# Hybrid decoder block on eight cores: one input tile held back, PSUM copies moved to VectorE, LayerNorm statistics paced at two a step

## The reference

```python
u = rms_norm(h, mix_pre_g)
proj = u @ w_in                                  # 1024 -> 5120
u_glu = proj[..., :2048]; p = proj[..., 2048:3072]
gates = sigmoid(proj[..., 3072:])                # g_conv, g_pool
y_conv = conformer_conv_branch(u_glu, ...)       # GLU, depthwise conv 31, LayerNorm, swish, @ w_conv_out
y_pool = pooling_branch(p, ...)                  # trailing means 2, 4, 8, 16 minus token, group linear, @ w_pool_out
h = h + rms_norm((g_conv * y_conv + g_pool * y_pool) @ w_o, mix_post_g)
v = rms_norm(h, mlp_pre_g)
v = square(relu(v @ w_ff1)) @ w_ff2
h = h + rms_norm(v, mlp_post_g)
```

## Time and profile before

| | us |
|---|---|
| median of the runs shown | 975.74 (975.29 to 1109.9) |
| the profiled execution | 976.0 |
| its span on the slowest core (7) | 974.4 |
| spans of the eight cores | 971.7 to 974.4 |
| TensorE busy on core 7 | 949.2 (97%) |
| VectorE busy | 451.3 (46%) |
| ScalarE busy | 277.6 (28%) |

### The profile page before, as it was taken

How to read it: one execution, slowest core, us unless ns; L and a number is a source line. 1 busy time by engine, 2 the same in 40 slices (tenths; PEclk the granted TensorE clock), 3 DMA queues, 4 the chain that set the end, 5 groups by cost and what they waited for, 6 DMA issues and landing times.

```text
span 974.4 us, 14114 instructions; the slowest of 8 cores (971.7 to 974.4 us)
## 1 busy us (share of the span) xinstructions
PE 949.2 (97%) x4971; PEld 484.2 (50%) x4971; DVE 451.3 (46%) x767; ACT 277.6 (28%) x531; POOL 62.6 (6%) x112
## 2 busy tenths in 40 slices
PE   7789999999999999999999999999999999999996
PEld 4655666665545544444444444444444444444444
DVE  4478886575482114566666630344223431244222
ACT  4553111132114431333335530233202330133211
POOL 1010001000010000121213200000000000000000
PEclk9999999999999999999999999999999999999999
DMA  9995165976780021759989995220022001210021
GB/s 183 253 146 74 17 89 105 143 109 115 118 140 1 1 87 15 143 117 191 168 190 178 196 197 90 87 87 1 1 87 87 1 1 44 87 43 1 1 86 66
DMA packets 93111, 91.21 MB, mean 94 GB/s; under 512 B 43601, under 2 KB 74577, under 8 KB 92914
## 3 DMA queue, kind: packets, MB, share of 16 engines
q0 software_dynamic: 32416, 35.13, 26.2%
q1 hardware_dynamic: 60626, 55.18, 21.1%
HBM read 98.88 MB, written 16.84 MB: 119 GB/s over the span
## 4 chain that ended last, share of the span: by engine, by line
PE 91%; DMA 3%; DVE 3%; ACT 1%; issue 1%; DVEq 0%; ACTq 0%; SPq 0%
PE ps L220 90%; DMA arena<-w_in 2%; DMA arena<-xh 1%; ACT arena L238 1%; PE ps L223 1%; DVE arena L246 1%; DVE arena L250 1%; DVE arena L477 0%; DMA arena<-arena 0%; DVE arena L241 0%; ACT sm L238 0%; DVE arena L256 0%; DVEq L159 0%; DVE sm L400 0%; ACTq L159 0%
## 5 line engine op out<-in xcount | busy, mean ns | idle before, releaser
L220 PE MATMUL ps<-arena 128*128 128x512 bf16 (+4 forms) x4731 | 937.9, 360 | 13.9 <-DVE arena L246 2.8
L220 PEld LDWEIGHTS ps<-arena 128*128 128x128 bf16 (+1 forms) x4731 | 470.1, 103 | 473.4 <-issue 25.7
L238 ACT ACTIVATE arena<-ps 128x512 bf16<-128x512 f32 (+5 forms) x346 | 203.0, 593 | 622.1 <-PE ps L220 467.0
L246 DVE TENSOR_SCALAR ps<-ps 128x512 f32<-128x512 f32 x128 | 89.1, 699 | 110.9 <-PE ps L220 110.2
L241 DVE TENSOR_TENSOR ps<-ps,arena 128x512 f32<-128x512 f32 (+1 forms) x65 | 43.6, 688 | 176.1 <-ACT arena L238 175.6
L250 DVE SCALAR_TENSOR_TENSOR arena<-arena,ps 128x512 bf16<-128x512 f32 (+1 forms) x64 | 43.9, 686 | 133.0 <-ACT arena L238 111.0
L241 DVE TENSOR_TENSOR arena<-ps,arena 128x512 bf16<-128x512 f32 (+2 forms) x52 | 42.3, 830 | 35.6 <-ACT arena L238 29.6
L238 ACT ACTIVATE arena<-arena 128x1024 bf16<-128x1024 f32 (+1 forms) x33 | 34.8, 1054 | 46.3 <-DVE arena L250 35.8
L250 DVE SCALAR_TENSOR_TENSOR arena<-ps,sm,arena 128x512 f32<-128x512 f32 (+1 forms) x65 | 45.1, 737 | 5.0 <-DVE sm L400 3.0
L250 DVE SCALAR_TENSOR_TENSOR arena<-arena,sm 128x1024 bf16<-128x1024 f32 (+1 forms) x33 | 42.3, 1282 | 4.3 <-POOL sm L396 2.4
L241 DVE TENSOR_TENSOR arena<-arena 128x512 bf16<-128x512 f32 (+2 forms) x56 | 38.4, 690 | 4.3
(11 more groups left out here) (34 smaller groups left out, 91.3 us busy)
## 6 DMA issues: line engine op xcount, KB each, us to landing
arena<-xh SPq DMA_DIRECT2D x32, 512.0 KB, 8.6
arena<-w_ff POOLq DMA_DIRECT2D x16, 1024.0 KB, 27.8
out<-arena SPq DMA_DIRECT2D x31, 512.0 KB, 3.1
arena<-out SPq DMA_DIRECT2D x16, 512.0 KB, 4.1
arena<-w_in POOLq DMA_DIRECT2D x12, 512.0 KB, 13.1
arena<-w_in POOLq DMA_DIRECT2D x2, 2048.0 KB, 17.2
arena<-gb SPq DMA_DIRECT2D x4, 512.0 KB, 6.4
arena<-w_pool_out POOLq DMA_DIRECT2D x2, 1024.0 KB, 23.1
```

Source lines behind the costliest of these rows:

```text
L220: kb.op("pe", lambda e: e.matmul(o, lhsT=l, rhs=r, start=start, stop=stop), [l, r], [o])
L238: kb.op("act", lambda e: e.activation(out=o, in_=i, func=func, **kw), rd, wr)
L246: kb.op("dve", lambda e: e.tensor_scalar(out=o, in0=a, scalar1=s1, scalar2=s2, op0=op0, **kw), rd, [o])
```

## The change

Three edits. SyncE issues x tile 0 (the third after 2 and 3) only when tile 3 has landed. All copies of the units with u = 2 and 3 go to VectorE; in the same list of calls, the 14 warm matmuls ahead of unit (0,1) become 6 ahead of it and 8 behind unit (1,1), and units (2,1) and (3,1) come before the transposes of tiles 1 and -1. The background queue gives up two items a step in place of three.

```diff
-                          after=[wev[j - 4]] if j in (4, 5, 6) else [])
+                          after=[wev[j - 4]] if j in (4, 5, 6) else [xev[3]] if j == 0 else [])
...
-                p_group(cc, 256 * u, 256, "dve" if u > 1 and cc % 2 else "act")
+                p_group(cc, 256 * u, 256, "dve" if u > 1 else "act")
...
-        do([(warm, 6), (nrm, 2), (setup,), (nrm, 3), (trn, 2), (warm, 3), (nrm, 0), (trn, 3), (nrm, 1), (nrm, -1), (warm, 14),
-            (pu, 0, 1), (pu, 1, 1), (trn, 0), (trn, 1), (trn, -1), (pads,), (pu, 2, 1), (pu, 3, 1),
+        do([(warm, 6), (nrm, 2), (setup,), (nrm, 3), (trn, 2), (warm, 3), (nrm, 0), (trn, 3), (nrm, 1), (nrm, -1), (warm, 6),
+            (pu, 0, 1), (pu, 1, 1), (warm, 8), (trn, 0), (pu, 2, 1), (pu, 3, 1), (trn, 1), (trn, -1), (pads,),
             (pu, 0, 0), (pu, 1, 0), (pu, 2, 0), (pu, 3, 0), (pu, 4, 1), (pu, 4, 0), (nrm, 4), (pu, 5, 1), (pu, 5, 0),
             (nrm, 5), (pu, 6, 1), (pu, 6, 0), (pu, 7, 1), (trn, 4), (pu, 7, 0), (trn, 5), (nrm, 6),
             (pu, 0, 2), (pu, 1, 2), (pu, 2, 2), (nrm, 7), (trn, 6), (pu, 3, 2), (pu, 4, 2), (nrm, 8), (pu, 5, 2),
...
-                pump(3)
+                pump(2)
```

## The result

The changed kernel takes 982.91 us (median of 981.4 to 983.55) where the kernel before, run beside it on the same chip, takes 975.67: a ratio of 1.0073, with a 95% interval of 1.0053 to 1.0093. By the ratio the change costs 7.1 us (0.1% is 0.98 us); the forecast was 974.4, in a range of 972.0 to 977.8. The profiled execution took 983.55 us. The changed kernel is slower, clear of noise, though by less than 2%.

A forecast was written before the change was run, and what follows sets the result against it. TensorE was taken to set the pace from 58 us, so an earlier start of the 512-token blocks moves the end. Slowest span 1.3 us shorter: 976.0 - 1.3 - 0.26, about 974.4 us; range 972.0 to 977.8.

The forecast's parts named there:

- Part 1: Holding x tile 0 until tile 3 lands: first weight piece at 15.5 to 16 us, second unchanged; no gain so far.
- queued behind it: On SyncE behind held x tile 0: tiles 1 and -1, vec, and tile 4, which waits for the first weight piece anyway.
- S: Start of the third token block, unit (0,2): 38.42 us before on core 7, forecast 37.55; core 4 forecast 37.75.
- 400 packets: Weight packets brought forward in 1.5 us of having the engines alone, worth 1.2 us at the full rate.
- Part 2: New projection order: unit (6,1) at 31.4 us on core 7, 0.6 later; earlier tile 4 still brings the third token block forward.
- half clock at (2,1): Rival, chance 0.1: 1.5 us TensorE idle after transpose 0 halves the clock at unit (2,1), costing 1.3 us; time 975.7.
- Part 3: Eight copies moved from ScalarE to VectorE: third token block to 512-token blocks 17.9 us against 19.74, 1.9 us less.
- G: Start of the 512-token projection blocks: 58.16 us before on core 7, forecast 55.45; core 4 56.67, forecast 55.65.
- Nothing: Rival, chance 0.1: transposes of tiles 8 to 11 land when they did; core 4's 512-token blocks do not move; 975.7.
- The idle at *G: Rival, chance 0.15: idle ahead of the 512-token blocks shrinks from 2.64 to 2.0 us, clock stays full; 1.3 us more, 973.1.
- Part 4: Two statistics a step, four moved into the last two steps: price 0, at most 1.4 us if VectorE's idle were gone.

The follow-up runs named there:

- the hold alone: Kernel before, with only x tile 0's issue held until x tile 3 has landed: 979.26 us, ratio 1.0031.
- order alone: Kernel before, with only the new order of warm matmuls (6 ahead of unit (0,1), 8 behind (1,1)), units and transposes: 978.16 us, ratio 1.0027.
- order with all 14: Kernel before, with units (2,1), (3,1) ahead of the transposes of tiles 1 and -1, all 14 warm matmuls still ahead of (0,1): 976.58 us, ratio 1.0008.
- the copies alone: Kernel before, with only the copies of units u = 2 and 3 all on VectorE: 977.22 us, ratio 1.0012.
- memsets: Kernel before, with sixteen small one-element memsets added on VectorE and nothing else: 978.04 us, ratio 1.0028.

## Why the prediction was wrong

- **The failed step: Part 1, "queued behind it".** The prediction listed what stands behind the held transfer on SyncE, and stopped there. The waiting goes on: behind the transfer stands ScalarE's square, behind it VectorE's reciprocal and product, and behind these, on VectorE, tile 3's copy, for which unit (0,1) waits. "Their transposes now stand behind more work" was true of tile 0's own and said nothing of tile 3's. Instead of about 16 us, (0,1) started at 21.32, and *S* came at 44.38 instead of 37.55. In the changed kernel, moving tile 3's copy ahead brought 5.0 of the 7.1 us back; with the hold alone the late tiles' transposes, ahead of (2,1), took its place.
- **Part 1, the size of the delay.** "Later by one to three us" for tile 0; it is 5.6: the chain has it from 9.40 to 17.30, 7.9 us in flight, beside 3.4 us for a tile into idle queues, and before it was in at 11.7. While it is in flight the weights move too, and they gain what the tiles lose: SyncE issues tile 4, which waits for the first piece, at 12.27 us, 5.0 earlier than before (17.27) and ahead of the bounds of 13.8 to 17.2. The "400 packets" were too few. The second piece stayed, as said (19.3 to 20.7).
- **Part 2.** From (2,1) to (6,1) it takes 10.8 us (27.53 to 38.33) and from there to *S* 6.05; the prediction had 10.85 and 6.15, and the copy wait of 0.85 us at (0,0) is there. Right in itself, on a start that was 7 us late.
- **The rival "half clock at (2,1)"** was the right kind and got 0.1. Its place was wrong (ahead of (0,1), not behind it) and so was its price: the 24 matmuls took 5.92 us where full clock makes them 3.6: 2.3 us, not 1.3. Moving eight warm matmuls behind (1,1) costs 1.9 us by itself (order alone against order with all 14). The rule of the Trainium skill that the prediction named ("TensorE: Matmul & The Clock Gate", Part 1: the throttled clock is the default, activity lifts it) agrees: 0.50 behind the idle of 3.76 us that six warm matmuls leave.
- **Part 3** came out in the changed kernel, in part by luck: *S* to *G* is 18.03 us (17.9 forecast, 19.74 before), VectorE is busy 16.52 of these 18.1 us, the wait of 2.35 us on ScalarE is gone, the idle ahead of *G* is 2.31 us. But this is at an *S* nearly 7 us late, with the DMA engines at 0.70 in that stage against 1.02 before. At about the *S* that was forecast (the copies alone, 36.5 to 38.6 us) tile 8's transpose landed 4 to 5 us later after *S*, and 17.9 held on two cores of eight. The rival "Nothing" describes core 4 there: tile 8's transpose lands at 52.81 us, before at 52.84, and *G* moves by 0.2 us. The idle at *G* did not drop enough: 2.1 to 2.5 us, with the half clock on six cores of eight behind it, as before. What failed is the claim that the stages behind *G* stay as long as before: the moved copies shift VectorE's pause into the eight scalings. No row of the prediction showed TensorE's idle there, though its 1.85 us were in the trace, right behind the last of the earlier trace rows.
- **Part 4** was right: price 0.
- **The range.** Each rival was priced alone and added to a start taken as safe. Its upper end, 977.8, holds one mishap; here the queue, the clock and the pause came together. The sum for core 7 misses by 62.41 - 55.45 = 7.0 us at *G* and by 3.3 us behind it (919.6 against 916.3).

## What to carry to other kernels

A wait added to a transfer must be followed through every engine that works on the data: on each, look at what stands behind the consumer in that engine's queue, not only behind the transfer in its own. Where TensorE waits 1 to 2 us for a run of small instructions at the seam of two stages, give that run one group more of cover: it was worth 1.8 us here, more than all three edits were meant to bring, and it makes the kernel deaf to shifts in another engine's stream. Matmuls that only keep the clock up are work like any other; count the idle that opens when they are moved, and the time they take where they now stand.

## What the runs showed of the hardware

VectorE stands still for some 0.4 us (0.23 to 0.47, from the end of the entry before) at entries of its recorded stream that lie 128 apart, where no operand is awaited. So a few instructions more early on move these pauses, and with them a stall hundreds of microseconds later. The Trainium skill ("Runtime: NRT & Kernel Launch", Instruction fetch mechanics) says that an engine's instructions are refilled in blocks of 256 while it runs, and that crossing a block is mostly hidden. The trace has the pauses at half that distance, and the one at 242 us is plainly not hidden; that the refill is its cause no run here shows.

At the seam of the two stages an idle of TensorE of 1.85 or 1.86 us was followed by the full clock on all 64 cores that have it (before and seven experiments). One of 2.20 to 2.23 us was followed by the half clock on 14 of 40 (after, copies alone, memsets, and the change without the hold or with tile 3 first). That costs the core about 1.6 us more: in copies alone, from the first convolution matmul behind this idle to TensorE's next idle, of 1.23 us near 355 us, cores 0, 4 and 7, with the half clock, take 120.6 us, the other five 119.0.
